# Gated linear attention in the token blocks of a decoder step: projections in the weight stream, the recurrence tile by tile

## The reference, cut to what matters

```python
bg, cg, hin, q, k, v, r, ga, gb, alow = jnp.split(h @ w_in, points, axis=-1)
y_conv, new_buf = short_conv(cg * hin, conv_buf, conv_w, conv_b)
branch_a = (bg * y_conv) @ w_proj_a
log_a = jax.nn.log_sigmoid((alow @ w_alpha + b_alpha).astype(jnp.float32)) / GLA_GATE_TAU
...
o, s_new = gla_chunked(qh, kh, vh, ah, gla_state)      # 4 heads, keys 128, values 256
o = rms_norm(o.astype(h.dtype), gla_norm_w.reshape(GLA_HEADS, GLA_HEAD_V))
o = o.reshape(bsz, t, GLA_DV) * jax.nn.silu(r)
branch_b = o @ w_proj_b
merged = jax.nn.sigmoid(ga) * branch_a + jax.nn.sigmoid(gb) * branch_b
return merged @ w_out, new_buf, s_new.astype(gla_state.dtype)
```

```python
o_inter = jnp.einsum('bhcd,bhde->bhce', qi * jnp.exp(cum), s)
scores = jnp.einsum('bhid,bhjd,bhijd->bhij', qi, ki, decay)
o = o_inter + jnp.einsum('bhij,bhje->bhie', scores, vi)
s_new = jnp.exp(last[:, :, 0, :])[..., None] * s + jnp.einsum('bhjd,bhje->bhde', ki * jnp.exp(last - cum), vi)
```

## Time and profile before

| | |
|---|---|
| median of 3 runs | 4790.31 us (4782.79 to 4793.29) |
| the profiled execution | 4796.1 us, its span 4794.3 us |
| TensorE, VectorE, ScalarE, GpSimd busy | 70%, 55%, 17%, 35% |
| gathers' queue, ordinary queue | 59.5% and 14.8% of the 16 DMA engines' time |
| mean granted clock of TensorE | 0.772 |

### The profile page before, as it was taken

One profiled execution on the slowest core, in us unless ns is written; L12 is line 12 of the kernel. 1 busy time (PEld: TensorE's weight loads), 2 busy tenths in 40 slices (PEclk: granted clock), 3 DMA queues, 4 the chain that ended last, 5 costly groups with the idle time before them and its releaser, 6 DMA issues. The chain is left out here.

```text
span 4794.3 us, 46337 instructions
## 1 busy us (share of the span) xinstructions
PE 3340.5 (70%) x15679; PEld 1703.1 (36%) x15679; DVE 2624.4 (55%) x7543; ACT 805.6 (17%) x1284; POOL 1669.0 (35%) x1379
## 2 busy tenths in 40 slices
PE   8688996864358676586658856758666666677676
PEld 2578885864225444152115533314300011111111
DVE  0355345315865354577866444557688555555555
ACT  1222222323112211311001311121100001000000
POOL 0311100643225444354325534434333333333332
PEclk9789988986669888697779978769866666666666
DMA  6211111544369898998879988999899899999998
GB/s 248 87 36 37 46 38 36 168 147 136 150 247 367 319 352 329 372 380 347 314 275 404 405 326 343 394 361 398 334 355 362 354 408 404 406 409 416 404 415 353
DMA packets 243428, 1400.13 MB, mean 292 GB/s; under 512 B 30661, under 2 KB 47685, under 8 KB 100986
## 3 DMA queue, kind: packets, MB, share of 16 engines
q0 software_dynamic: 156672, 1140.92, 59.5%
q1 hardware_dynamic: 86522, 256.22, 14.8%
HBM read 1345.59 MB, written 51.43 MB: 291 GB/s over the span
## 5 line engine op out<-in xcount | busy, mean ns | idle before, releaser
L999 DVE CUSTOM_DVE_ANT_0 peer_uv<-peer_uv,all_PS 128x512 f32<-128x512 f32 x2176 | 1435.7, 685 | 1172.3 <-DMA peer_uv<-in_uv,peer_idx 762.6
L938 PE MATMUL all_PS<-peer_hT,peer_sel 96*128 96x512 bf16 x2176 | 1012.6, 489 | 1111.4 <-DVE peer_halves L999 914.6
L921 POOL DMA_INDIRECT peer_uv<-in_uv,peer_idx x1088 | 1060.7, 975 | 1800.8 <-PE all_PS L957 1408.3
L938 PEld LDWEIGHTS all_PS<-peer_hT,peer_sel 96*128 96x128 bf16 x2176 | 203.3, 103 | 2095.1 <-DVE peer_halves L999 1679.6
L957 PE MATMUL all_PS<-peer_uv,peer_zw 128*32 128x512 f32 x4352 | 881.4, 857 | 2.7 <-DVE peer_zw L1019 2.7
L809 POOL TENSOR_TENSOR flow_w_lo<-flow_w,flow_w_hi 128x1024 fp32r<-128x1024 f32 (+1 forms) x204 | 459.5, 2258 | 505.7 <-ACT flow_w_hi L802 503.4
L973 ACT ACTIVATE peer_ge<-peer_pre 128x4 f32<-128x4 f32 x272 | 55.6, 205 | 2119.0 <-DVE peer_pre L1005 2027.1
L829 PE MATMUL all_PS<-mix_h_hi,flow_w_hi 128*128 128x384 f32 (+1 forms) x672 | 278.5, 414 | 31.7 <-POOL flow_w_lo L809 31.7
L802 ACT ACTIVATE flow_w_hi<-flow_w 128x1024 fp32r<-128x1024 f32 (+1 forms) x204 | 203.7, 1004 | 435.8 <-DMA flow_w<-in_w_proj_a 118.3
L831 PE MATMUL all_PS<-mix_h_hi,flow_w_lo 128*128 128x384 f32 (+1 forms) x672 | 225.7, 336 | 0.0
L830 PE MATMUL all_PS<-mix_h_lo,flow_w_hi 128*128 128x384 f32 (+1 forms) x672 | 225.6, 336 | 0.0
(11 more groups left out here) (277 smaller groups left out, 4800.1 us busy)
## 6 DMA issues: line engine op xcount, KB each, us to landing
cond_w<-in_w_ada SPq DMA_DIRECT2D x12, 2048.0 KB, 8.0
flow_w<-in_w_gate_ab SPq DMA_DIRECT2D x48, 512.0 KB
flow_w<-in_w_query SPq DMA_DIRECT2D x48, 512.0 KB
flow_w<-in_w_conv SPq DMA_DIRECT2D x36, 512.0 KB
peer_uv<-in_uv,peer_idx POOLq DMA_INDIRECT x1088
gla_w<-in_w_heads SPq DMA_DIRECT2D x24, 512.0 KB, 3.7
flow_w<-in_w_proj_b SPq DMA_DIRECT2D x24, 512.0 KB
flow_w<-in_w_out SPq DMA_DIRECT2D x24, 512.0 KB
```

The costliest lines, as they stand in the source:

```text
L921: self.nc.gpsimd.indirect_dma_start(out=self.uv[:, n % self.NUV, :], out_offset=None, in_=self.A["uv"], in_offset=bass.IndirectOffsetOnAxi ...
L938: nc.tensor.matmul(PS[:, f, :], self.sel[:, c:c + 1].broadcast_to([3 * GR, P]), self.hT[:, g % self.NH, f * 512:(f + 1) * 512], start=True ...
L999: nc.vector.tensor_tensor_reduce(part, part, PS[:, f, :], 1.0, 0.0, ALU.mult, ALU.add, self.halves[:, d, f, e:e + 1]).then_inc(M["dotted"], 1)
```

## The change

It removes `heads_phase`, `project3` and `split`, and the on-chip copies `h_hi` and `h_lo` of all tokens. In each block `mix_phase` gets a step for the low-rank gates and 24 weight blocks in 24 steps ahead of the convolution (q, k, two for v, r twice for each head), and writes q and k, v, and r with its gate and norm gain to memory by tile. A new `chain_phase` follows: for each tile of the block the log gates of all heads, then the heads in turn, then the norm of all heads together. Its exponents go through bank BE in two parts and through BM for the third, its scores through bank BS in two halves; E, Q, K, sT, kT have one buffer each. The state S of all heads stays on the chip from block to block. SHARES has seven entries. In addition `merge_phase`, `norm_phase` and `keys_phase` use fewer or smaller buffers, `merge_phase` reads the recurrence's output tile by tile, and in the stages' first instructions `gat.gelu` and `gat.dots` stand ahead of the copies of the inputs.

```diff
-SHARES = (94, 50, 38, 42, 90, 100)
+SHARES = (170, 100, 50, 38, 42, 90, 100)
...
-            condition_phase(nc, A, G)
-            heads_phase(nc, A, G)
+        condition_phase(nc, A, G)
...
+                once = ([A["w_heads"][i, b] for i in range(H) for b in range(6)] + [A["w_conv"][c, q] for c in range(CC) for q in range(3)] + ...
...
+                        with Scope(nc, f"rank{part.index}") as rank:
+                            low = rank.sb("low", [RANK + 1, part.n])
+                            mix_phase(nc, A, G, part, gat, w, w0, a_in, low, marks[0], marks[1])
+                            chain_phase(nc, A, G, part, gat, low, marks[1], marks[2])
...
 def mix_phase:
-        h = Halves(sc, "h", KD, n, lambda g: A["h1"][part.index, :, 4 * g:4 * g + 4, 0:n], 4)
+        h = Halves(sc, "h", KD, n, lambda g: A["h1"][part.index, :, 2 * g:2 * g + 2, 0:n], 2)
+        steps = [("low", 0, 0, 0)]
+        steps += [(name, i, e, 6 * i + b) for i in range(H)
+                  for name, e, b in (("q", 0, 0), ("k", 1, 1), ("va", 0, 2), ("vb", 1, 2), ("r", 0, 4), ("r", 1, 5))]
...
+                    for t, u in enumerate(part.tiles):
+                        where = A["qk"][u, :, i, :, 0:R[t]] if name == "k" else A["rg"][u, :, 2 * i:2 * i + 2, 0:R[t]]
+                        sp.dma_start(where, out[:, p % 2, :, part.at[t]:part.at[t] + R[t]]).then_inc(saved[p % 2], 16)
...
+def chain_phase(nc, A, G, part, gat, low, lo, hi):
...
+        turns = Turns(lo, hi, 10 * nt)
...
+            def exponents(m):
+                for part_of, (b, at, l0, l1) in enumerate(((BE, 0, 0, 4), (BE, 0, 4, 8), (BM, 0, 8, 9))):
+                    if part_of == 1:
+                        pe.wait_ge(M["e_exp"], 3 * m + 1)
...
+            def scores(m):
+                pe.wait_ge(M["qk_done"], 3 * m + 3)
+                if m:
+                    pe.wait_ge(M["o_out"], m)
+                nc.tensor.transpose(PS[:, BM, P:2 * P], K[:, LV, :], ident[:, :]).then_inc(M["t_mm"], 1)
+                for half in range(2):
+                    if m or half:
+                        pe.wait_ge(M["masked"], 2 * m + half)
+                    for l in range(4 * half, 4 * half + 4):
+                        last = nc.tensor.matmul(PS[0:n, BS, l % 4 * P:l % 4 * P + n], lhs, rhs, start=True, stop=True)
+                    last.then_inc(M["s_mm"], 1)
...
+                for i in range(H):
+                    gat.spread(pe, turns.upto(10 * t + 1 + 2 * i))
+                    scores(m0 + i)
+                    if i + 1 < H:
+                        exponents(m0 + i + 1)
+                    gat.spread(pe, turns.upto(10 * t + 2 + 2 * i))
+                    results(m0 + i)
...
+                for i in range(H):
+                    gat.dots(dve, turns.upto(10 * t + 1 + 2 * i))
+                    reduce(m)
+                    gat.dots(dve, turns.upto(10 * t + 2 + 2 * i))
+                    if kind[t]:
+                        state(m)
+                    if i + 1 < H:
+                        decay(m + 1)
+                    if not kind[t]:
+                        state(m)
...
 def merge_phase:
-        o = Halves(sc, "o", KD, n, lambda g: A["ob"][part.index, :, g, :, 0:n], 2)
+        o = Tiles(sc, part, A["ob"])
...
+            gat.gelu(act, turns.before())
             a.make_high(nc, act)
             for g in range(o.groups):
                 o.make_high(nc, act, g)
-            gat.gelu(act, turns.before())
...
 def keys_phase:
-        raw = sc.sb("raw", [P, nt, KD, P])
+        raw = sc.sb("raw", [P, 2, KD, P])
```

More of the change, by code:

```diff
@@ L123, in block @@
         return self.engines.enter_context(self.nc.Block())
[L126 to L144, removed]
 def norm_squares(nc, act, s, src, sq, ready=None, chunks=range(KD)):
@@ L216, in condition_phase @@
         small_in, w_in = sc.sem("small_in"), [sc.sem(f"w_in{b}") for b in range(NBUF)]
-        sig, silu, w_used, r_out, t_mm, mod_out, own, ready, done, high, low = (sc.sem(n) for n in (
-            "sig silu w_used r_out t_mm mod_out own ready done high low").split())
+        sig, silu, w_used, r_out, t_mm, mod_out, own, ready, done = (sc.sem(n) for n in (
+            "sig silu w_used r_out t_mm mod_out own ready done").split())
         ns = norm_sems(sc)
@@ L1077, in mix_phase @@
         block = sc.block()
         bank = lambda j: PS[:, FRONT + j % 4, 0:n]
-        by_act = lambda j: j >= NCONV or j % 3 == 0
-        acts = lambda j: sum(by_act(i) for i in range(j + 1))
-        vecs = lambda j: sum(not by_act(i) for i in range(j + 1))
+        by_vec = [name == "r" or name == "conv" and q > 0 for name, _, q, _ in steps]
+        by_act = [not (name == "conv" and q > 0) for name, _, q, _ in steps]
+        acts, vecs = (lambda j: sum(by_act[:j + 1])), (lambda j: sum(by_vec[:j + 1]))
@@ L1082, in mix_phase, with coming, pair, stored_before @@
         turns = Turns(lo, hi, NJ)
+        def coming(j):
+            name, _, _, b = steps[j]
+            return {"low": (), "va": (), "vb": (w0 + b + w.pairs, w0 + b + 1 + w.pairs)}.get(name, (w0 + b + w.pairs,))
+        def pair(j):
+            name, i, _, _ = steps[j]
+            return 2 * i + (name == "r") if name in "qkr" else 2 * H + i
+        def stored_before(p):
+            return 16 * sum(nt if q < 2 * H else 1 for q in range(p % 2, p, 2))
         @block.sync
         def _(sp):
-            for g in range(h.groups):
+            sp.dma_start(lw[:], A["w_low"]).then_inc(lw_in, 16)
+            for g in range(h.slots):
@@ L1241, in _ @@
             gat.turn(sp, turns.before())
+            for g in range(1, o.groups):
+                o.fetch(sp, g)
             for j in range(NJ):
@@ L1280, in _ @@
         def _(dve):
+            gat.dots(dve, turns.before())
             a.make_low(nc, dve)
@@ L1283, in _ @@
                 o.make_low(nc, dve, g)
-            gat.dots(dve, turns.before())
             for j in range(NJ):
```

973 lines of the change are left out of this document (493 added, 480 removed).

## The result

The changed kernel took 4958.9 us (median of 4, 4954.2 to 4964.1) against 4791.8 us (4782.8 to 4794.4) in the same comparison: a ratio of 1.035 [1.033, 1.037], 167 us slower. The forecast was 5075 us, 283 us slower than the kernel before.

What follows compares the result with a forecast made beforehand. Dense work and gathers mostly add in blocks 1 and 2; transfers bind the last stretch. 168 + 901 + 1400 + 1572 + 1036 = 5077 us of span, forecast 5075; own range 4960 to 5180, 8 in 10 4860 to 5270.

Steps and rivals of the forecast that it cites:

- The frame: Whole kernel: the time is a sum of stretches one behind the other, with the last stretch staying at 1036 us.
- The forecast's balance: Heads' work: three thirds in the blocks cost 348 + 306 + 296 = 950 us where 667 went.
- Projections and recurrence: Each block: projections add 101 us in block 0, 110 in the others; recurrence adds 242 and 203 us.
- the count of 9.0 us: Recurrence: one head of one prompt tile takes 9.0 us, 6.1 of it VectorE's work, the rest holes and hand-overs.
- The token price: Blocks 1 and 2: each gathered token adds 1.74 and 1.78 us to the dense work after the change.
- for 384 columns I take 559 us: Blocks 1 and 2 before the change: dense work without gathers, scaled from block 0's 553 us for 320 columns.
- at lower densities I go down the same line: Blocks 1 and 2: token price falls from 1.81 and 1.87 us to 1.74 and 1.78 at densities 0.33 and 0.43.
- I give them nothing: Conditioning: removing the high and low copies on ScalarE and GpSimd saves no time.
- The smaller edits: Stage inputs in smaller pieces and first dot products ahead of them: +5 us a block, bounds -15 to +35.
- the gathers cover it: Rival for blocks 1 and 2: extra dense work fills gaps between transfers, full cover giving 4479 us; chance 0.12.
- the chain overlaps nearly as well as before: Rival for the recurrence: three tiles take 130 us in place of 203, about 4865 us in all; chance 0.06.
- the signs: Profile checks: block 1 above 1350 us, last stretch from near 4040, transfers' share 0.75 to 0.8, shorter waits for gathers.

Runs made afterwards that it cites:

- the half runs: Kernel before and changed kernel, each with only half the gathers in blocks 1 and 2, the rest in the last stretch: 4898.1 and 5128.9 us.
- b_serial: Kernel before with all gathers of blocks 1 and 2 left to the last stretch: 5195.7 us, ratio 1.086.

## Why the prediction was right, and what it had wrong

**The frame held.** The end is a sum of stretches, the last one did not change (1040 for 1036), and the heads' work done three times cost more than once: 380 + 328 + 332 = 1040 us of dense work where 667 + 17 went. Of the 1040, 193 were covered. The forecast's balance is of the times with the gathers in them, 950 against 667, and measured it is 844 against 690: the same sign, 283 us more where 154 came. The errors did not all point one way: the start was 23 us early and block 0 was 32 late (a few us of both are the cut between them), blocks 1 and 2 were 77 and 61 shorter.

**Projections and recurrence held, among gathers too.** 103 us for 101; alone, the recurrence of three prompt tiles took 207 and 196 for 203. In block 0 it took 272 for 242: the log gates of its three tiles begin at 386.5, 451.2 and 514.6 us and the stage ends at 639, so the start took 17 us (forecast 14), the prompt tiles 64.7 and 63.4 (forecast 61 each) and the sample tile 124 (forecast 106, though 14 + 11 and four heads of 21 are 109); two of its heads take 26.8 us each. Here is one head of a prompt tile in block 0 of the kernel after, from first mask to first mask (start, duration, engine, line, idle before in brackets):

```profile
403.06 0.69 DVE L1159 TENSOR_TENSOR chain_prod<-all_PS,chain_pairs 128x512 f32<-128x512 f32 x1 [2.40 <-PE all_PS L987]
...
405.91 0.69 DVE L1159 TENSOR_TENSOR chain_prod<-all_PS,chain_pairs 128x512 f32<-128x512 f32 x1 [2.17 <-PE all_PS L987]
...
406.64 1.91 DVE L1163 TENSOR_REDUCE chain_sT<-chain_prod 128x128 f32<-128x1024 f32 x1
...
409.54 0.15 DVE L1145 COPY chain_decayed<-chain_E 128x1 f32<-128x1 f32 x1 [0.99 <-ACT chain_E L1074]
...
414.44 0.69 DVE L1159 TENSOR_TENSOR chain_prod<-all_PS,chain_pairs 128x512 f32<-128x512 f32 x1 [2.02 <-PE all_PS L987]
```

The windows of this head and of one of the next tile, from first mask to first mask (columns of the earlier trace rows):

```profile
403.06:414.44 11.38, 8.70 (x29) 6.61 (x29) 6.18 (x9) 2.02 (x5) 0.00 (x0) 0.50 0.01 1
479.43:488.07 8.64, 5.32 (x33) 4.09 (x33) 6.26 (x10) 2.02 (x5) 0.00 (x0) 0.99 0.00 1
```

The six periods in the two tiles are 8.6 to 11.5 us (forecast 9.0), and they follow the granted clock: 11.4 and 11.5 at 0.50, 9.9, 9.9 and 9.3 at 0.81 to 0.83, 8.6 at 0.99. In the head shown the three holes are in the forecast's places but longer: 2.17 us for the second four scores (forecast 1.2), 0.99 for the exponents (0.7), 2.02 for the next head's first four (0.8). In the head at 0.99 they are 1.25, 0.10 and 1.00 us. So the count of 9.0 us is that of the upper level of the clock, 2.4 GHz, and the forecast's bound of 12 us is about what the lower, 1.2 GHz, gives; the truth lay between. The clock of the whole recurrence of block 0 was 0.56 for 0.89 before; ahead of the two slowest heads (381 to 401 us and 451 to 467) TensorE was busy a quarter of the time, at 0.50. One reading of the forecast was wrong without hurting it: each score product leaves two records, sixteen for the eight of a head in a tile, so the fourteen of the earlier trace rows are seven products, not fourteen.

**The token price was mis-sized.** The two steps that failed are "for 384 columns I take 559 us", measured 509, and "at lower densities I go down the same line", 1.74 and 1.78 us, measured 1.64 and 1.74. In block 1 the first makes 48 us (885 for 837) and the second the other 29 of the 77 by which it came out shorter; in block 2 they make 47 and 14 of 61. The first error has its root in one trace: from it I could not separate dense work from tokens, and took block 0's choosing of experts with a guess for its gathers. A base 50 us too high also made the price at the densities of before too low, 1.81 and 1.87 for 1.98 and 2.00. The second error is the straight line. Drawn through the two measured prices it is flatter still: at 0.35 and 0.46 it gives 1.95 and 1.96 us, and blocks of 1414 and 1595 us, further off than the 1400 and 1572 of the forecast. So part of the nearness of 1.74 and 1.78 is luck, the two errors against each other; both prices of before lie where the curve is flat, and only the half runs show it bend.

**The conditioning and the small edits.** "I give them nothing" was wrong by 15 us at the same point (17 by the windows), 12 to 13 of which are VectorE's wait for GpSimd. The smaller edits I took at +5 us a block; the order of the first turn in them is worth -21 over all, and the rest of them isn't separated.

**The rivals and the signs.** That the gathers cover it is refuted: the share of the transfers fell to 0.79 and 0.83 in place of rising to 0.95. It was right in part, 193 us of the 660 that went among gathers, and short of the 283 that the forecast named for parity; by the measured dense times it would have taken 1040 - 684 = 356. That the chain overlaps nearly as well as before is refuted too: three prompt tiles alone took 196 and 207 us, not 130. Of the signs, the share of the transfers fell to about what was named (0.75 to 0.8), and the waits for landed gathers fell well below 109 and 198; block 1 took 1323 us where "more than 1350" was named, and the last stretch began at 3912 us, not near 4040, as both blocks were shorter. The sentence of the Trainium skill (Perfetto Trace Analysis, Optimization Strategy), that interleaving regimes may help, holds for the gathers themselves: b_serial is 404 us slower than before. It did not hold for taking more work into the blocks.

**The tables.** The recurrence's table loads in block 0 of the kernel after (busy us, mean ns, idle before):

```profile
L1091 ACT ACT_TABLE_LOAD x3 | 3.8, 1283 | 0.1
L1074 ACT ACT_TABLE_LOAD x3 | 3.8, 1283 | 5.0 <-PE all_PS L967 5.0
L1122 ACT ACT_TABLE_LOAD x3 | 3.8, 1283 | 0.1
L1125 ACT ACT_TABLE_LOAD x3 | 3.8, 1283 | 0.1
```

Logarithm (L1091, L1122) and exponential (L1074, L1125) again have a load each, four a tile, as the forecast's "four or five" had it. The Trainium skill (ScalarE: Activation LUTs, section on table sets) has both in one set; the measurement decides, as it did in the forecast.

## What to carry to other kernels

Before you move work beside gathers, measure two kernels: one with nothing woven in and one with half. They give the dense time and show whether the price of a gather falls with more dense work around it; here neither could be read from the woven trace alone. Work that is done once for all tokens and is cut into blocks has to be covered by at least what the cutting adds; here 193 us were, and 356 were needed. Put what is ready ahead of what waits for its input at the head of every stage.

## What the runs showed of the hardware

An elementwise operation of GpSimd on SBUF made a VectorE operation that takes 0.41 us take 1.96 to 2.19; eight of them moved the whole kernel by 12 us, in either direction. The granted clock of the recurrence was 0.56 in block 0 and 0.61 and 0.69 in blocks 1 and 2 with no gathers among its steps, and 0.72 to 0.74 with them. One head of a prompt tile with no gathers took 11.4 to 11.5 us at 0.50 (the lower level, 1.2 GHz) and 8.6 us at 0.99 (the upper, 2.4 GHz); VectorE's own work in it was the same, 6.2 and 6.3 us. TensorE was busy 114 of 207 us in block 1 without gathers and 221 of 332 with 86 of them; how much the chain's own products gained there by the higher clock isn't measured apart.
